# GLA scores with a 128 column stationary, decay logits with 128 rows, in a hybrid encoder step

## The chip, the cores and the metric

The kernel runs on one core of a Trainium2 chip. The metric is the device time of one execution in microseconds. Three runs of the kernel before took 977.99, 978.71 and 979.06 us, a median of 978.71. A further execution was profiled: it took 978.32 us.

The engines are named as the profile names them: PE is TensorE's matmul, PEld its load of the stationary operand, DVE VectorE, ACT ScalarE, POOL GpSimd, SP the engine that issues the DMAs.

## The reference

One layer over 2048 prompt frames (one stream) and 64 frames of a running stream, all in float32, model width 1024. RMSNorm, one input projection of 2832 columns, and then three groups whose outputs are gated, joined and sent through one output projection: banded attention (512 wide), gated linear attention or GLA (256) and a depthwise convolution of width 31 (256). The change is in GLA, which the reference writes in chunks of 64 frames:

```python
log_a = jax.nn.log_sigmoid((glr @ gla_w_up + gla_b).astype(jnp.float32)) / GLA_TAU
...
def step(S, inp):
    qc, kc, vc, gc = inp
    b = jnp.cumsum(gc, axis=1)
    b_last = b[:, -1:]
    q_t = qc * jnp.exp(b)
    k_t = kc * jnp.exp(-b)
    A = jnp.where(causal, jnp.einsum('bthd,bshd->bhts', q_t, k_t), 0.0)
    o = jnp.einsum('bhts,bshv->bthv', A, vc) + jnp.einsum('bthd,bhdv->bthv', q_t, S)
    k_end = kc * jnp.exp(b_last - b)
    S = jnp.exp(b_last[:, 0])[..., None] * S + jnp.einsum('bshd,bshv->bhdv', k_end, vc)
    return S, o
```

There are 4 heads with 32 key and 64 value columns each. `glr` has 16 columns. The first line is the "logits of the decay", `A` the "scores".

## The kernel before

The program for each engine is written by hand in its order, with semaphores between them; nothing is planned by a scheduler. Products in float32 are split: an operand becomes a high and a low part in a reduced format (names in `hi`/`lo`, `h`/`l`), and three matmuls stand for one. The small products of GLA aren't split; each is one float32 matmul, which the profile shows as two records on PE and two on PEld.

There are two passes. Pass A (up to about 480 us) does attention for 17 tiles of 128 frames and writes its part of the output. Pass B does GLA and the convolution in eight blocks b = 0 to 7 of 256 frames. Block 0 also carries the 64 frames of the running stream as a third tile, so it is 320 wide. In pass B of block b, TensorE does in this order (`for b in range(NB + 1)`, L2132 to L2215):

- the projections for the convolution (`project_b`, L1805) and for the values (`project_v`, L1958), with transposes of the block before between them,
- `gg` j = 0, the low-rank transpose `lowrank_T` (L2065), `gg` j = 1, then `gate_logits` (L2074), then `cg` and `pointwise` (L2055), `gk`, `gq`,
- the output of the block before in four halves (`output_b`, L1973, twelve matmuls each), and between them `kend_T` (L2081), `scores` for tiles 0 and 1 (L2098 and L2101), `state_update` (L2111) and `gla_o` (L2124, L2127).

A tile holds two chunks. `scores(b, i)` makes both chunks' scores of tile i for all 4 heads, in one bank of 512 columns: the left 256 for the first chunk (64 query columns a head), the right 256 for the second, whose stationary operand holds the keys of both chunks. The keys stand in `kb[128, 2, 5, 64]`, five groups of 64 columns for each tile: group 0 has the first chunk's keys for the first chunk's queries, groups 1 and 2 both chunks' keys for the second's, groups 3 and 4 those for the state. For the first chunk only 64 keys matter, so its stationary has 64 columns and its output 64 rows. VectorE's `mask_scores` then copies under a mask: rows 0 to 63 of the left half (L1624), all of the right half (L1627), and `gla_o` needs that (`a_masked`). The moving operand `qbd` has each head's queries in its own 32 rows and zeros elsewhere, so one matmul serves four heads.

`gate_logits` multiplies `wup` (16 rows of weights, one of bias) with `glrT`, the 17 rows of the transposed low-rank part with its row of ones. ScalarE puts these there (`take_lowrank`, L1122). `glrT` is the upper part of `bb`, where VectorE later writes the block's sums of the decay, all 128 rows (L1580). `wup` is a view of the packed parameters, which are in memory with 128 rows, zero below the 17th.

GpSimd clears some tiles once, ahead of block 0 (L881 to L885), and counts them on `zeros_b`; PE (L2061), ACT (L1230), DVE (L1740) and GpSimd itself (L916) wait for this count.

VectorE's order in a block is set by the convolution: 62 taps (L1478, L1482), cut into portions, with the steps of GLA, the adds of the output (`add`, L1653) and the split of the next block's input (L524) between them.

Of the kernel before, what the change touches and what calls it, by code (L numbers as in the profile page):

```python
# [25 lines left out]
ACT = mybir.ActivationFunctionType  # L26
# [7 lines left out]
P = 128  # L34
# [3 lines left out]
DEC = 64  # L38
CHUNK = 64
# [4 lines left out]
GH, GK, GV, LR = 4, 32, 64, 16  # L44
# [39 lines left out]
PARAMS, N_PARAMS = {}, 0  # L84
for _name, _width, _rows in (("reset", WIDE // 4, P), ("mask", P, P), ("wpw", CJ * CD, P), ("convw", CJ * CW, P),
                             ("convp", 3 * CJ, P), ("uh", CJ * HIST, P), ("glagain", 1, P), ("bpw", CJ, P),
                             ("wup", P, LR + 1), ("sts", GH * GV, P)):
    PARAMS[_name] = (N_PARAMS, _width, _rows)
    N_PARAMS += _width

# [25 lines left out]
def width(b):  # L116

    return WIDE if b == 0 else 256


def groups(b):

    if b < 0 or b >= NB:
        return []
    return [(0, 0, 256, (0, 1)), (1, 256, DEC, (2,))] if b == 0 else [(b + 1, 0, 256, (0, 1))]
# [7 lines left out]
def tiles(b):  # L133

    return [i for _, _, _, own in groups(b) for i in own]
# [59 lines left out]
def build(nc, ins, consts, x_T, outs):  # L195
# [7 lines left out]
    def sb(name, shape, dt=F32, ctx=es):  # L203
        return ctx.enter_context(nc.sbuf_tensor(name, shape, dt))

    def sem(name):
        return es.enter_context(nc.semaphore(name))

    with es:
# [68 lines left out]
        bb = sb("bb", [P, WIDE])  # L278
# [11 lines left out]
        zm = sb("zm", [P, WIDE])  # L290
        ez = sb("ez", [P, WIDE])
        qt = sb("qt", [P, WIDE])
        glrT = bb[0:LR + 1, :]
        e1, e2, e3 = qt, zm, ez
        eL = sb("eL", [P, 5])
        dec = sb("dec", [P, 3])
        kb = sb("kb", [P, 2, 5, 64])
        kbs = sb("kbs", [P, 2, 64])
        qbd = sb("qbd", [P, GH, WIDE])
# [21 lines left out]
        wup, glagain, bpw, sts = part("wup"), part("glagain"), part("bpw"), part("sts")  # L321
# [5 lines left out]
        T = [es.enter_context(nc.psum_tensor(f"T{i}", [P, 512], F32)) for i in range(3)]  # L327
# [40 lines left out]
        consts_a, consts_b, zeros_a, zeros_b = sem("consts_a"), sem("consts_b"), sem("zeros_a"), sem("zeros_b")  # L368
# [21 lines left out]
        gv_taken, lr_psum, lr_T = sem("v_taken"), sem("lowrank_psum"), sem("lowrank_T")  # L390
# [301 lines left out]
        def on_y(g):  # L692

            gi, _, w, own = g
            buf = on[:, own[0]:own[-1] + 1, :].rearrange("p i n -> p (i n)")
            return buf[:, 0:CJ * w].rearrange("p (j n) -> p j n", n=w)
# [143 lines left out]
        def _(pool):  # L840
# [42 lines left out]
            nc.gpsimd.memset(qbd[:, :, :], 0.0).then_inc(zeros_b, 1)  # L883
            nc.gpsimd.memset(glr1[:, :, LR:LR + 1], 1.0).then_inc(zeros_b, 1)
            nc.gpsimd.memset(eps_3[:, :], EPS).then_inc(zeros_b, 1)  # L885

            def o_rinv(g):
                gi, _, w, own = g
                a, e = own[0] * GH, own[-1] * GH + GH
                rows = slice(0, min(w, P))  # L890
                pool.wait_ge(go_ss, gi + 1)
                need(pool, go_n, gi)
                nc.gpsimd.tensor_tensor(oms[rows, a:e], oss[rows, a:e], eps_h[rows, a:e], ALU.add).then_inc(go_ms, 1)  # L893
                pool.wait_ge(go_ms, gi + 1)
                nc.gpsimd.tensor_tensor(orr[rows, a:e], oms[rows, a:e], mhalf[rows, a:e], ALU.pow).then_inc(go_r, 1)
# [17 lines left out]
                pool.wait_ge(gate_mul, at + 1)  # L913
                nc.gpsimd.tensor_tensor(dst, dst, graw[n % 2][:, 0:w], ALU.add).then_inc(gate_done, 1)

            pool.wait_ge(zeros_b, 5)  # L916
            for b in range(NB + 1):
                for g in groups(b - 1) if b < NB else []:
                    o_rinv(g)
# [11 lines left out]
        def _(act):  # L931
# [155 lines left out]
            def o_square(g):  # L1087
                gi, _, w, own = g
                rows = slice(0, min(w, P))
                bank = T[0] if own == (2,) else S[1]  # L1090
                act.wait_ge(go_psum, go_count(g))
                need(act, cnT_psum, groups_before(max(gi - 1, 0)))
                nc.scalar.activation(on[rows, own[0]:own[-1] + 1, :], bank[rows, 0:256 * len(own)].rearrange(
                    "p (i n) -> p i n", n=256), ACT.Square).then_inc(go_sq, 1)
# [24 lines left out]

            def take_lowrank(b):  # L1120
                act.wait_ge(lr_psum, b + 1)
                nc.scalar.activation(glrT[:, 0:width(b)], T[0][0:LR + 1, 0:width(b)], ACT.Copy).then_inc(lr_T, 1)  # L1122

            def log_decay(b):
                w = width(b)
# [58 lines left out]
            for b in range(NB + 1):  # L1184
                cur, done = b < NB, groups(b - 1) if b < NB else []
                for g in done:
                    o_square(g)
                if cur and b > 0:
                    glu_tanh(b, 0)
                    glu_tanh(b, 1)  # L1190
                if b == 1:
                    act.wait_ge(A.out_psum, 2 * TILES)
                    split_hi(B, OUT_HI, OUT_HI + 2)
                for g in done:
                    y_hi(g, on_y(g), ybg, 4.0, yg_ready, yg_hi)
                for i in tiles(b):
                    take_v(b, i)
                    if (b, i) == (0, 0):
                        split_hi(B, 5 * STAGES, 6 * STAGES)
                if b == 0:  # L1200
                    act.wait_ge(A.y_lo, 2 * TILES)
                    split_hi(B, 3 * KT, 4 * KT)
                if cur:
                    take_gate(b, 0)
                    take_lowrank(b)
                for g in done:
                    if g[3] != (2,):
                        conv_silu(g)
                if cur:
                    take_gate(b, 1)  # L1210
                    log_decay(b)
                for g in done:
                    if g[3] == (2,):
                        conv_silu(g)
                if cur:
                    if b == 1:
                        split_hi(B, OUT_HI + 2, OUT_HI + 4)
                    take_gate(b, 2)
                    decays(b)
                    if b == 1:  # L1220
                        split_hi(B, OUT_HI + 4, OUT_HI + 6)
                    take_gate(b, 3)
                    if b == 1:
                        split_hi(B, OUT_HI + 6, OUT_HI + 8)
                for g in done:
                    y_hi(g, cl[:, :, g[1]:g[1] + g[2]], ybc, 0.25, yc_ready, yc_hi)
                if cur:
                    take_kend(b)
                    if b == 0:
                        act.wait_ge(zeros_b, 5)  # L1230
                    q_blocks(b)
                if b == NB - 1:
                    g = groups(b)[0]
                    conv_silu(g)
                    o_square(g)
                    y_hi(g, cl[:, :, 0:256], ybc, 0.25, yc_ready, yc_hi)
                    y_hi(g, on_y(g), ybg, 4.0, yg_ready, yg_hi)
                if b + 1 < NB:
                    split_pair_hi(b + 1, 0)
                    split_pair_hi(b + 1, 1)  # L1240
# [3 lines left out]
        def _(dve):  # L1244
# [416 lines left out]
            for b in range(NB + 1):  # L1661
                p = b - 1
# [74 lines left out]
                if cur:  # L1737
                    taps(7)
                if b == 0:
                    dve.wait_ge(zeros_b, 5)  # L1740
                if prev:
                    add(p, 0, 1)
                if cur:
# [45 lines left out]
        def _(pe):  # L1789
# [268 lines left out]

            def lowrank_T(b):
                if b == 0:  # L2060
                    pe.wait_ge(zeros_b, 5)  # L2061
                pe.wait_ge(gv_taken, 2 * (tile_no(b, 0) + len(tiles(b))))
                for i in tiles(b):
                    rows = DEC if i == 2 else P
                    last = nc.tensor.transpose(T[0][0:LR + 1, i * P:i * P + rows], glr1[0:rows, i, :],  # L2065
                                               ident[0:rows, 0:rows])
                last.then_inc(lr_psum, 1)
# [19 lines left out]
            def scores(b, i):  # L2087
                bank = S[0] if i == 1 else T[2]
                by_head = lambda ap: ap.rearrange("p (h n) -> p h n", n=CHUNK)
                pe.wait_ge(qbd_ready, b + 1)  # L2090
                if i == 0:
                    need(pe, yc_ready, groups_before(b))
                elif i == 1:
                    need(pe, cn_ready, groups_before(b))
                else:
                    pe.wait_ge(a_masked, 1)
                first = kbs[:, 0, :] if i == 2 else kb[:, i, 0, :]
                last = nc.tensor.matmul(by_head(bank[0:64, 0:256]), first, qbd[:, :, i * P:i * P + CHUNK], start=True,  # L2098
                                        stop=True)
                if i < 2:  # L2100
                    last = nc.tensor.matmul(by_head(bank[:, 256:512]), kb[:, i, 1:3, :].rearrange("p c n -> p (c n)"),  # L2101
                                            qbd[:, :, i * P + CHUNK:(i + 1) * P], start=True, stop=True)
                last.then_inc(a_psum, 1)
# [28 lines left out]
            for b in range(NB + 1):  # L2132
                p = b - 1
# [147 lines left out]
```

## Time and profile before

| | us |
|---|---|
| median of 3 runs | 978.71 |
| the profiled execution | 978.32 |
| its span | 976.5 |
| PE busy (share of the span) | 920.2 (94%) |
| PEld busy | 813.5 (83%) |
| DVE busy | 790.8 (81%) |
| ACT busy | 475.2 (49%) |
| POOL busy | 203.9 (21%) |

The span runs from the first to the last instruction of the profiled execution; the 1.8 us between it and the time lie around it. Shares of busy time are means over two quite different passes, so the place of the change has to be read in its own window. The chain that ended last is the page's way to say what set the end: from the last instruction back, at each step to whatever released it. `128*64` in a row is a stationary of 128 rows and 64 columns, `128x256` the moving operand. Starts on PE overlap: a matmul is issued before the one ahead of it has ended, so what a matmul costs is the distance from its start to the next start, which the chain's pieces give, and not its duration.

### The profile page before, as it was taken

The page shows a single profiled execution, that of the slowest core. Times are in us where ns is not written, and L with a number is a line of the kernel's source. Part 1 is how long each engine was busy: PE and PEld are TensorE (multiplying, and loading weights), DVE is VectorE, ACT ScalarE, POOL GpSimd, SP SyncE. Part 2 cuts the span into 40 slices and gives each one's busy share as a digit, 9 for nine tenths or more (in the row PEclk, how much of TensorE's full clock was granted, in tenths as well). Part 3 has the DMA queues.
Part 4 walks back from the last instruction along what each step waited for, and adds up shares of the span by engine and source line. Part 5 has one row for each costly group of instructions (what it writes and reads, how often), then busy time and mean ns, then how long its engine had stood idle before and what let it go on. Part 6 is the DMA issues. An engine that isn't in the chain of part 4 may idle for free.

```text
span 976.5 us, 15956 instructions
## 1 busy us (share of the span) xinstructions
PE 920.2 (94%) x5713; PEld 813.5 (83%) x5713; DVE 790.8 (81%) x1905; ACT 475.2 (49%) x1166; POOL 203.9 (21%) x250
## 2 busy tenths in 40 slices
PE   5889999999999999998988789999999999999987
PEld 4767888888888888887975777998989898998965
DVE  6778888888888888888897768778878888888984
ACT  7666666666666666776642152041423224142311
POOL 1332222222222222210030230120301112120310
PEclk9899999999999999998997899999999999999999
DMA  9532332222222332163502203212040211203021
GB/s 297 201 125 88 109 108 107 97 103 105 107 95 95 105 108 87 62 198 90 153 23 77 66 24 97 76 44 87 2 130 1 76 54 61 70 13 119 1 76 57
DMA packets 57839, 87.79 MB, mean 90 GB/s; under 512 B 10048, under 2 KB 34496, under 8 KB 57760
## 3 DMA queue, kind: packets, MB, share of 16 engines
q1 hardware_dynamic: 57760, 86.77, 27.4%
q8 instruction: 46, 0.75, 0.3%
q14 instruction: 33, 0.27, 0.1%
HBM read 60.21 MB, written 26.60 MB: 89 GB/s over the span
## 4 chain that ended last, share of the span: by engine, by line
PE 74%; DVE 14%; ACT 4%; issue 3%; DMA 3%; SPq 1%; POOL 1%; POOLq 0%; DVEq 0%; ACTq 0%
PE J L656 19%; PE J L1805 17%; PE J L1973 9%; PE J L671 9%; DVE acc L1482 6%; PE J L1958 3%; PE S L1860 3%; PE S L2127 1%; PE T L1895 1%; PE T L2055 1%; ACT sc L1004 1%; PE S L1918 1%; DMA x_normed_scratch<-xraw 1%; ACT whi L462 1%; PE J L1995 1%
## 5 line engine op out<-in xcount | busy, mean ns | idle before, releaser
L1482 DVE SCALAR_TENSOR_TENSOR acc<-ub,cwh,acc 128x256 f32<-128x256 f32 (+1 forms) x480 | 225.1, 533 | 0.2
L656 PE MATMUL J<-whi,xhi 128*128 128x512 f32 (+1 forms) x408 | 151.3, 371 | 10.0 <-DVE wlo L472 10.0
L1805 PE MATMUL J<-xbh,whi 128*128 128x256 f32 (+1 forms) x512 | 150.9, 295 | 4.5 <-issue 4.5
L656 PE MATMUL J<-wlo,xhi 128*128 128x512 f32 (+1 forms) x408 | 147.6, 362 | 0.0
L656 PE MATMUL J<-whi,xlo 128*128 128x512 f32 (+1 forms) x408 | 147.3, 361 | 0.0
L1805 PE MATMUL J<-xbl,whi 128*128 128x256 f32 (+1 forms) x512 | 146.9, 287 | 0.0
L1805 PE MATMUL J<-xbh,wlo 128*128 128x256 f32 (+1 forms) x512 | 146.8, 287 | 0.0
L1805 PEld LDWEIGHTS J<-xbh,whi 128*128 128x128 f32 x512 | 97.8, 191 | 7.6 <-issue 7.1
L1805 PEld LDWEIGHTS J<-xbl,whi 128*128 128x128 f32 x512 | 98.0, 191 | 0.2
L1805 PEld LDWEIGHTS J<-xbh,wlo 128*128 128x128 f32 x512 | 97.7, 191 | 0.0
L656 PEld LDWEIGHTS J<-whi,xhi 128*128 128x128 f32 x408 | 78.2, 192 | 20.8 <-DVE xlo L614 10.0
L656 PEld LDWEIGHTS J<-whi,xlo 128*128 128x128 f32 x408 | 78.0, 191 | 12.8
L656 PEld LDWEIGHTS J<-wlo,xhi 128*128 128x128 f32 x408 | 78.2, 192 | 10.6
L1004 ACT ACTIVATE sc<-sc,nmx 128x192 f32<-128x192 f32 x136 | 60.3, 446 | 10.4 <-DVE nmx L1302 10.3
L1296 DVE CUSTOM_DVE_ANT_0 sc<-S,bias,sinks 128x192 f32<-128x192 f32 (+2 forms) x136 | 50.2, 406 | 10.2 <-PE S L1860 10.2
L671 PE MATMUL J<-whi,yhi 128*128 128x512 f32 x136 | 56.4, 415 | 0.0
L671 PE MATMUL J<-wlo,yhi 128*128 128x512 f32 x136 | 53.7, 395 | 0.0
L671 PE MATMUL J<-whi,ylo 128*128 128x512 f32 x136 | 53.6, 394 | 0.0
L604 POOL TENSOR_TENSOR xraw<-xraw,rb 128x1024 f32<-128x1024 f32 x17 | 40.8, 2400 | 51.4 <-ACT rb L598 51.4
L893 POOL TENSOR_TENSOR oms<-oss,eps_h 128x8 f32<-128x8 f32 (+1 forms) x9 | 4.9, 549 | 179.9 <-DVE oss L1495 179.0
L1958 PE MATMUL J<-whi,xbh 128*128 128x272 f32 x136 | 40.6, 298 | 0.4 <-DVE ub L1260 0.4
L1805 PE MATMUL J<-xbh,w2hi 128*128 128x256 f32 (+1 forms) x128 | 37.6, 294 | 3.1 <-ACT cgate L1118 3.1
(270 smaller groups left out, 2264.7 us busy)
## 6 DMA issues: line engine op xcount, KB each, us to landing
out<-res SPq DMA_DIRECT2D x60, 256.0 KB, 2.0
x_normed_scratch<-xraw SPq DMA_DIRECT2D x17, 512.0 KB, 2.9
xraw<-xT SPq DMA_DIRECT2D x16, 512.0 KB, 3.5
xtok<-in_x_prompt SPq DMA_DIRECT2D x16, 512.0 KB, 3.6
res<-in_x_prompt SPq DMA_DIRECT2D x16, 512.0 KB, 4.5
xbraw<-x_normed_scratch SPq DMA_DIRECT2D x16, 512.0 KB, 5.2
res<-out SPq DMA_DIRECT2D x14, 512.0 KB, 4.2
wraw<-in_w_in SPq DMA_DIRECT2D x52, 128.0 KB, 2.5
```

The lines of the kernel that those rows point to most:

```text
L462: nc.scalar.activation(weights(col, width)[0], stage(stage_of(ps, n))[:, 0:width], ACT.Copy, scale=scale).then_inc(ps.whi, 1)
L604: nc.gpsimd.tensor_tensor(xraw[t.par][:, :, :], xraw[t.par][:, :, :], rb[:, :].unsqueeze(1).to_broadcast([P, KT, P]), ALU.mult).then_inc(x ...
L656: last = nc.tensor.matmul(bank[:, 0:width], x[x_slot(ps, t)][:, k, :], w, start=(k == 0 and n == 0), stop=(k == KT - 1 and n == 2))
L671: last = nc.tensor.matmul(bank[:, :], y[:, k, :], w, start=(k == 0 and n == 0), stop=(k == 3 and n == 2))
L1004: last = nc.scalar.activation(unit(u), unit(u), ACT.Exp, bias=nmx[:, u:u + 1], accum_out=esum[:, u:u + 1])
L1296: nc.vector.tensor_tensor_reduce(out=unit(u)[:, cols], in0=S[n % 2][:, c * BAND:(c + 1) * BAND][:, cols], in1=bias[:, n, cols], scale=1.0, ...
L1482: nc.vector.scalar_tensor_tensor(acc[:, j, 0:frames], src, w, acc[:, j, 0:frames], ALU.mult, ALU.add).then_inc(conv_step, 1)
L1805: last = nc.tensor.matmul(bank[:, 0:w], wt, x[:, k, 0:w], start=(k == 0 and m == 0), stop=(k == KT - 1 and m == 2))
L1860: last = nc.tensor.matmul(S[n % 2][:, c * BAND:(c + 1) * BAND], qT[:, n, c, :, :].rearrange("p e q -> p (e q)"), band(t, n // 2, o, c), st ...
L1895: last = nc.tensor.transpose(T[2 * g][:, c * 256 + n % 2 * P:c * 256 + n % 2 * P + P], sc[:, n, c * 256:c * 256 + P], ident[:, :])
L1958: last = nc.tensor.matmul(bank[:, 0:B.widths[1]], x[:, k, at:at + P], wt, start=(k == 0 and m == 0), stop=(k == KT - 1 and m == 2))
L1973: last = nc.tensor.matmul(bank[:, :], y[:, k % 2, at:at + P], wt, start=(k == 0 and m == 0), stop=(k == 3 and m == 2))
```

## The change

The first chunk's scores of tiles 0 and 1 get a stationary of 128 columns, groups 0 and 1 of `kb`, and write 128 rows instead of 64. Rows 64 to 127 of the left half then hold products that nobody reads. The third tile of block 0 keeps 64 columns.

The logits take all 128 rows of `wup` and of `bb`. Rows 17 to 127 of `wup` are zero. Those of `bb` must hold finite numbers: GpSimd clears `bb` once, and from block 1 on it holds the sums of the block before. The count on `zeros_b` goes from 5 to 6, and ScalarE waits for it in block 0 before it writes `bb`. No other instruction is added, none changes its place, and no transfer changes.

```diff
@@ -84,7 +84,7 @@
-                             ("wup", P, LR + 1), ("sts", GH * GV, P)):
+                             ("wup", P, P), ("sts", GH * GV, P)):
@@ -290,7 +290,7 @@
-        glrT = bb[0:LR + 1, :]
+        glrT = bb[:, :]
@@ -883,6 +883,7 @@
             nc.gpsimd.memset(eps_3[:, :], EPS).then_inc(zeros_b, 1)
+            nc.gpsimd.memset(bb[:, :], 0.0).then_inc(zeros_b, 1)
@@ -913,7 +914,7 @@
-            pool.wait_ge(zeros_b, 5)
+            pool.wait_ge(zeros_b, 6)
@@ -1119,7 +1120,9 @@
                 act.wait_ge(lr_psum, b + 1)
-                nc.scalar.activation(glrT[:, 0:width(b)], T[0][0:LR + 1, 0:width(b)], ACT.Copy).then_inc(lr_T, 1)
+                if b == 0:
+                    act.wait_ge(zeros_b, 6)
+                nc.scalar.activation(glrT[0:LR + 1, 0:width(b)], T[0][0:LR + 1, 0:width(b)], ACT.Copy).then_inc(lr_T, 1)
@@ -1227,7 +1230,7 @@
-                        act.wait_ge(zeros_b, 5)
+                        act.wait_ge(zeros_b, 6)
@@ -1737,7 +1740,7 @@
-                    dve.wait_ge(zeros_b, 5)
+                    dve.wait_ge(zeros_b, 6)
@@ -2058,7 +2061,7 @@
-                    pe.wait_ge(zeros_b, 5)
+                    pe.wait_ge(zeros_b, 6)
@@ -2094,8 +2097,9 @@
-                first = kbs[:, 0, :] if i == 2 else kb[:, i, 0, :]
-                last = nc.tensor.matmul(by_head(bank[0:64, 0:256]), first, qbd[:, :, i * P:i * P + CHUNK], start=True,
+                rows = slice(0, DEC if i == 2 else P)
+                first = kbs[:, 0, :] if i == 2 else kb[:, i, 0:2, :].rearrange("p c n -> p (c n)")
+                last = nc.tensor.matmul(by_head(bank[rows, 0:256]), first, qbd[:, :, i * P:i * P + CHUNK], start=True,
                                         stop=True)
```

## Rows read from the trace of the kernel before

**Rows 1.** The page, part 4: shares of the chain that ended last, by engine.

```profile
PE 74%; DVE 14%; ACT 4%; issue 3%; DMA 3%; SPq 1%; POOL 1%; POOLq 0%; DVEq 0%; ACTq 0%
```

**Rows 2.** Sums by window: length, busy us of PE, PEld, DVE, ACT, POOL, clock.

```profile
540.00:592.42 52.42, 41.63 (x293) 39.68 (x291) 38.71 (x85) 17.86 (x43) 17.21 (x16) 0.87 0.13 45
592.42:648.06 55.64, 55.64 (x371) 50.21 (x372) 43.71 (x104) 15.75 (x36) 7.74 (x10) 1.00 0.22 67
703.68:759.30 55.62, 55.62 (x396) 51.22 (x396) 46.05 (x109) 16.93 (x39) 9.47 (x12) 1.00 0.19 58
870.54:905.00 34.46, 34.46 (x231) 30.77 (x231) 28.09 (x67) 6.48 (x13) 3.87 (x4) 1.00 0.31 93
905.00:951.00 46.00, 42.00 (x279) 37.47 (x277) 41.49 (x97) 13.36 (x34) 11.85 (x12) 0.96 0.12 41
```

**Rows 3.** The chain in order of time (start us, us, what), outside the gapless stretch.

```profile
568.64 1.75 DVE acc L1482 x2
...
910.68 7.92 DVE acc L1482 x20
...
935.93 4.58 PE J L1973 x12
...
940.72 2.77 PE J L1973 x12
943.49 0.58 PE T L2098 x2
```

**Rows 4.** The chain in block b = 3.

```profile
715.16 0.57 PE T L2098 x2
715.73 0.63 PE T L2101 x2
716.36 0.58 PE S L2098 x2
...
720.33 0.86 PE T L2111 x4
...
748.34 2.84 PE J L1805 x24
751.18 0.62 PE T L2074 x2
751.81 3.04 PE J L1805 x24
```

**Rows 5.** Groups by shape, weight loads: shapes, count | busy us, mean ns | idle before.

```profile
L2101 PEld LDWEIGHTS T<-qbd,kb 128*128 128x128 f32 x16 | 2.4, 188 | 3.1 <-issue 3.1
...
L2074 PEld LDWEIGHTS T<-bb,params 17*128 17x128 f32 x16 | 2.3, 182 | 3.0 <-ACT bb L1122 2.0
...
L2098 PEld LDWEIGHTS T<-qbd,kb 128*64 128x64 f32 x16 | 1.5, 135 | 3.5 <-issue 2.5 <-ACT qbd L1155 1.0
```

**Rows 6.** Time line (start us, us, instruction, idle before): GpSimd's memset, transpose L2065.

```profile
480.27 0.31 POOL L881 MEMSET stp<- 128x256 f32 x1 [23.97 <-DVE ylo L1265]
...
493.34 0.86 POOL L912 TENSOR_TENSOR ggate<-ggate,graw 128x320 f32<-128x320 f32 x1 [10.68 <-ACT ggate L1118]
...
487.55 0.54 PE L2065 MATMUL T<-ident,glr 128*17 128x128 f32 x3
```

**Rows 7.** Time line, b = 0: the taps ahead of the masks, TensorE behind them.

```profile
519.88 2.05 DVE L1482 SCALAR_TENSOR_TENSOR acc<-ub,cwh,acc 128x350 f32<-128x350 f32 x4
...
522.76 0.67 PE L2124 MATMUL S<-stp,qt 128*128 128x256 f32 x2 [0.32 <-DVE asb L1627]
```

**Rows 8.** Time line, b = 7: the last mask, the transpose L2028.

```profile
947.53 0.43 DVE L1627 COPY_PREDICATED asb<-params,S 128x256 f32<-128x256 uint8 x1
...
948.50 0.60 PE L2028 MATMUL S<-ident,acc 128*128 128x128 f32 x4
```

**Rows 9.** Time line, b = 3: the state update and the matmul that reads it.

```profile
722.97 1.15 DVE L1639 SCALAR_TENSOR_TENSOR stp<-stp,dec,T 32x64 f32<-32x64 f32 x4
...
725.12 0.59 PE L2124 MATMUL S<-stp,qt 128*128 128x256 f32 x2
```

## The prediction, made before the kernel ran

> **What bounds the kernel now.** I read the page's chain first, then the sums by window, then the chain in order of time, then single instructions. On the page 74% of the chain that ended last runs on TensorE [rows 1]. Both edits act in the second half only (the mixer pass with its GLA part, eight blocks b = 0 to 7), so the question is in which blocks TensorE is the bound. The sums by window answer it. From 592.42 to 905.00 us TensorE is busy in every microsecond of every window, at a granted clock of 1.00. A block repeats in 55.62 us there, with 46.05 us of work for VectorE [rows 2]; the first, a middle and the last of six such windows stand there. Before it (b = 0, and b = 1 up to its output) and behind it (b = 7) TensorE has gaps [rows 2], and the chain runs through VectorE's convolution taps L1482, which cover the logits of b = 1 (the piece at 568.64 us) as those of b = 7 (the piece at 910.68) [rows 3].
>
> In one gapless block (b = 3) every piece of the chain is TensorE's. Five of them belong to this change: the scores L2098, L2101, L2098, L2101 with 0.57 + 0.63 + 0.58 + 0.63 = 2.41 us (the fourth repeats the second), and the logits of the decay, L2074, with 0.62 [rows 4]. What these take from start to start comes off the 55.62 us, if nothing else arrives late.
>
> **What a narrow or a short stationary costs.** The nearest full operation is L2111 (128 rows, 128 columns, 256 moving, float32): two matmuls in 0.86 us, 0.43 each [rows 4]. L2101 has exactly this shape and takes 0.63, though it waits for no semaphore; it only follows a matmul of 128*64. L2098 has half the columns to load, 135 ns against 188, and takes 0.57. The load queue shows where this goes. A load normally lies under the matmul before it. Before the loads of tile 0 of these two lines the queue stood idle for 3.5 + 3.1 = 6.6 us, and only 1.0 of it was a wait for another engine [rows 5]. So each change between a 64 column and a 128 column stationary uncovers a load and adds a pause.
>
> **Edit 1, scores with 128 columns** (tiles 0 and 1 of each block; the third tile of b = 0 keeps its 64). It takes 2.41 us out and puts four full matmuls in, 4 x 0.43 = 1.72. Saved: 0.69 us a block. Nothing in the trace shows a full load ahead of a full L2101, so I bound it: above, by L2111's 0.43 for all four; below, by 4 x 0.63 = 2.52, L2101 as it is now, a loss of 0.11 (rival C goes further). I take 0.43, since L2111 is the nearest in shape and type and L2101's only difference is what stands before it. The upper 64 rows that are now written are read by nobody, VectorE masks the same 64 rows as before, no instruction is added.
>
> **Edit 2, logits with 128 rows.** L2074 loads 17 rows and 128 columns. Its piece is 0.62 against 0.43: 0.19. The 24 matmuls behind it take 3.04 against 2.84 for the 24 ahead of it: 0.20 [rows 4]. The chain follows no other engine here, so this isn't a wait for ScalarE. Saved: 0.39 us a block; the bound from below is 0.00 (the load alone grows from 182 ns to 188 [rows 5]).
>
> Here two rules of the Trainium skill stand against each other. "TensorE: Matmul & The Clock Gate", section LDWEIGHTS, has a load paid by its columns and not by its rows: by that alone edit 2 gives nothing, and edit 1 makes each narrow load some 53 ns longer. The loads themselves agree with it (182 ns for 17 rows, 188 for 128, 135 for 64 columns), and it is what rivals A and C rest on. "TensorEngine Tiling (Array Packing)", section Key Properties, has TensorE drained whenever the tiling mode changes; by that both edits pay. The gaps around L2101 and L2074 agree with it, and it has no price.
>
> **What is added.** One memset of `bb`, 128x320, on GpSimd. That of `stp`, 128x256, took 0.31, so about 0.4 us. GpSimd was free 10.68 us before 493.34, at 482.66, so it ends near 483.1. The first that waits for the higher count is TensorE's transpose L2065, at 487.55 [rows 6]: 4.4 us of cover. ScalarE's new wait, ahead of the logits' input of b = 0, comes later still. I take both at 0; with the cover gone it is 0.4 us once.
>
> **In which blocks it counts.**
> - b = 2 to 6, both edits, no gap: 5 x (0.69 + 0.39) = 5.40 us.
> - b = 1: the scores lie in the gapless stretch, 0.69. Its logits lie beside taps that set the pace, 0 [rows 3].
> - b = 0: VectorE masks the scores after the taps that end at 521.93, and TensorE waits 0.32 us for the mask [rows 7]. 0 for both.
> - b = 7: the logits lie beside taps, 0. The scores are on the chain (943.49) [rows 3]. But the transpose L2028, at 948.50, also waits for the masks of both tiles, which VectorE ends at 947.53 + 0.43 = 947.96, at the pace of its taps and not of the scores [rows 8]. So it can come no earlier than about 948.05 and gains 0.45 of the 0.69. What follows moves with it.
>
> Sum: 5.40 + 0.69 + 0.45 = 6.54 us. The profiled execution took 978.32 us with a span of 976.5, which would become 971.8 and 970.0. The median of the runs shown, 978.71, is 0.39 above that execution; with it I get **972.2 us**.
>
> **What is late next.** The closest is VectorE's state update of tile 0, L1639. It ends at 722.97 + 1.15 = 724.12, and L2124, which reads it, starts at 725.12 [rows 9]. Of this 1.00 us the scores take 0.69, and 0.31 is left if VectorE doesn't move at all. It will move, since adds of the output ahead of it wait for TensorE. No new wait, but it is tight, and the next gain there would find it.
>
> **Rivals.**
> - A: rows don't matter. If 17 rows of stationary can be followed by 128 without a pause, and L2074's gaps have another cause, edit 2 gives nothing: 972.2 + 5 x 0.39 = 974.1 us. For it: its neighbours have the same 128 columns. Against it: 3.04 against 2.84 behind it, with no wait recorded. 12%.
> - B: VectorE takes over. If L1639 comes later than I think (its work falls together with GpSimd's in another way), six blocks give back about half of 0.69: 2.1 us, 974.3. For it: the slack of 0.31. Against it: VectorE has 9.6 us without work in a block. 5%.
> - C: slower. The pause comes not from the change of shape but from this strided `qbd` behind unrelated matmuls, and stays; then all that changes is the load. 188 - 135 = 53 ns, uncovered, four loads a block (two lines, two records), seven blocks on the chain: 1.5 us. Edit 2 then pays nothing either: 980.2 us. It decides as soon as the load isn't laid under the matmul ahead. For it: L2101's own loads are uncovered now. Against it: L2111, full and float32 too, runs at 0.43. 4%.
> - D: the clock. In b = 7 the first twelve L1973 take 4.58 us and the next twelve 2.77 [rows 3], after a gap, and this window has a granted clock of 0.96 [rows 2]. With other arrival times one such fall can be added, or this one can be missed: 1.8 us either way, 974.0 or 970.4. 6% for the worse.
>
> **Numbers.** My forecast has 73%, A 12, B 5, C 4, D 6. Faster by over 0.2% (2 us, about what a measurement of this kernel tells from none) means below 976.7, where all but C lie: faster 0.93, same 0.05, slower 0.02. The range reaches up past A, B and D (974.0 to 974.3) and leaves C out. Down it takes D's other sign with b = 7 at its full 0.69, 970.4 - 0.2. So 970.2 to 974.5.
>
> **What would show it.** L2098 and L2101 stand as 128*128, and the chain's pieces of scores sum to 1.7 us a block. L2074 is a 128*128 piece of 0.43 with 2.84 for the 24 behind it. A gapless block lasts 54.54 us, and the stretch before 592.4 keeps its length. L2028 of b = 7 waits for masks. I am wrong if L2101 stays at 0.63 (C), if L2074 keeps its gaps (A), or if TensorE waits for `stp` between 592 and 900 us (B).

## The result, and the profile after

The changed kernel takes 971.44 us (median of 4 runs, 970.4 to 973.35) against 978.88 (977.99 to 979.1) for the kernel before: a ratio of 0.9923, interval 0.9907 to 0.9939. The forecast was 972.2 us in a range of 970.2 to 974.5. A second sample of the changed kernel (e7) and the first together have a median of 972.55 over 12 runs.

The profiled execution took 970.40 us with a span of 968.6, 7.9 less than the span before. First the sums by window, cut at steps of one block from the start of the output of b = 1, in the columns of [rows 2] (after the clock come the busy share of the DMA engines and their GB/s):

```profile
540.00:591.00 51.00, 41.65 (x300) 40.09 (x298) 37.48 (x85) 17.86 (x44) 18.11 (x16) 0.90 0.13 45
591.00:645.53 54.53, 54.53 (x371) 50.75 (x372) 43.61 (x103) 15.67 (x36) 7.59 (x10) 1.00 0.22 68
700.07:754.60 54.53, 54.53 (x397) 51.78 (x396) 46.02 (x108) 16.85 (x39) 9.43 (x12) 1.00 0.19 59
863.65:898.11 34.46, 34.46 (x238) 32.00 (x236) 28.45 (x69) 6.48 (x13) 3.99 (x4) 1.00 0.30 92
898.11:944.00 45.89, 41.36 (x277) 38.07 (x276) 41.76 (x100) 13.36 (x34) 12.30 (x12) 0.96 0.12 41
```

The block without gaps lasts 54.53 us instead of 55.62. TensorE is still busy in all of it; its weight loads are busy for longer (51.78 against 51.22 us a block) in a shorter block, so the time did not come from less loading. The chain of b = 3 (start us, us, what) says where it came from:

```profile
711.56 0.43 PE T L2102 x2
711.99 0.43 PE T L2105 x2
712.42 0.43 PE S L2102 x2
712.85 0.43 PE S L2105 x2
...
744.05 2.84 PE J L1808 x24
746.89 0.43 PE T L2077 x2
747.32 2.83 PE J L1808 x24
```

These are the lines of [rows 4], three or four further down in the code. All four pieces of scores take 0.43 us, the figure of L2111, where they took 0.57 and 0.63. The logits take 0.43 for 0.62, and the 24 matmuls behind them 2.83 for 3.04. The groups of weight loads by shape show the gaps closed (busy us, mean ns | idle before):

```profile
L2105 PEld LDWEIGHTS T<-qbd,kb 128*128 128x128 f32 x16 | 3.0, 190 | 0.4
L2102 PEld LDWEIGHTS T<-qbd,kb 128*128 128x128 f32 x16 | 3.0, 188 | 0.7
L2077 PEld LDWEIGHTS T<-bb,params 128*128 128x128 f32 x16 | 2.5, 190 | 2.4 <-ACT bb L1125 2.4
```

L2102 now needs 188 ns to load instead of 135, and the queue stood idle 0.7 us before its sixteen loads instead of 3.5 [rows 5]. Before L2077 it was idle for 3.0 us, 2.0 of it a wait for ScalarE; what is left now is such a wait alone (2.4). The longer load costs nothing, since it lies under the matmul ahead again. Then b = 7, in the chain:

```profile
903.13 7.92 DVE acc L1485 x20
...
928.38 4.58 PE J L1976 x12
...
939.75 0.33 DVE asb L1627
940.08 0.34 DVE asb L1630
940.42 0.14 issue
940.55 0.63 PE S L2031 x4
```

The transpose L2031 waits for the last mask, as forecast. From the start of the output (928.38, before 935.93) to it (940.55, before 948.50 [rows 8]) 12.17 us pass instead of 12.57: a gain of 0.40.

The new memset of `bb` took 0.37 us and is over at 482.37. TensorE's transpose L2068, the first that waits for the higher count, starts at 486.96, and GpSimd's own next instruction at 493.10:

```profile
482.00 0.37 POOL L886 MEMSET bb<- 128x320 f32 x1
```

### The profile page after: what moved, and what is told of

Same layout as the page of the kernel before. It is cut to its first block, busy times and chain, and to the rows that moved or that the text cites. A ratio compares the mean times of both kernels' runs of the same rounds, so it can differ in the third digit from the quotient of the medians.

```text
span 968.6 us, 15958 instructions
## 1 busy us (share of the span) xinstructions
PE 911.9 (94%) x5713; PEld 818.6 (85%) x5713; DVE 789.7 (82%) x1905; ACT 474.2 (49%) x1166; POOL 204.9 (21%) x251
## 4 chain that ended last, share of the span: by engine, by line
PE 74%; DVE 13%; ACT 5%; DMA 3%; issue 3%; SPq 1%; POOL 1%; POOLq 0%; DVEq 0%; ACTq 0%
PE J L656 19%; PE J L1808 18%; PE J L671 9%; PE J L1976 8%; DVE acc L1485 6%; PE J L1961 3%; PE S L1863 3%; PE S L2131 1%; PE T L1898 1%; DMA wraw<-in_w_in 1%; PE T L2058 1%; ACT sc L1005 1%; ACT whi L462 1%; DMA x_normed_scratch<-xraw 1%; PE S L1921 1%
```

## The experiments

All medians are device us; one execution of each is profiled, and the length of a block is read in it from the start of one `kend` transpose (`kend_T`) to the next. The kernel before had a median of 978.90 to 979.14 us beside each group.

**One edit alone.** e1 has the full width scores and the short logits of before; e2 the reverse.

```diff
e1 (against before)
+                rows = slice(0, DEC if i == 2 else P)
+                first = kbs[:, 0, :] if i == 2 else kb[:, i, 0:2, :].rearrange("p c n -> p (c n)")
+                last = nc.tensor.matmul(by_head(bank[rows, 0:256]), first, qbd[:, :, i * P:i * P + CHUNK], start=True,
...
e2 (against before)
+                              ("wup", P, P), ("sts", GH * GV, P)):
...
+        glrT = bb[:, :]
...
+            nc.gpsimd.memset(bb[:, :], 0.0).then_inc(zeros_b, 1)
```

> Edit 1 alone. My theory (each change of shape between 64 and 128 columns costs about 0.1 us and uncovers a load): 0.69 us a block in b = 1 to 6, 0.4 in b = 7, so 4.5 us, a time of 974.3; a gapless block lasts 54.93 us. The 1.4 us that the changed kernel gained before 591 us in its profile stay away if they come from the logits of b = 1 (start of the output of b = 1 near 592.4 us, as before), and come if they are chance. Rival C (narrow operands cost by themselves, wider ones 53 ns more each): 980 us. Rival A says nothing here.

> Edit 2 alone. My theory: 0.39 us in each of b = 2 to 6, 1.95 us, a time of 976.9, a gapless block of 55.23 us. If in b = 1 the shorter logits let VectorE go on before GpSimd gets in (two taps of 0.95 us become 0.47 us), another 1.0 us: 975.9, with the output of b = 1 starting near 591.0 us. Rival A (rows don't matter): 978.9, gapless block 55.62.

e1: 975.51 us (6 runs), ratio 0.9965, interval 0.9951 to 0.9979; a block lasts 54.93 us, 0.69 less. e2: 978.74 us (12 runs), ratio 1.0003, interval 0.9991 to 1.0015; a block lasts 55.23 us, 0.39 less. So in the block the two gains are exactly the two terms of the forecast, and they add to the 1.09 of the changed kernel. In the whole time e1 stays 1.2 us behind the 974.3 expected, and the logits alone bring nothing that can be told (978.74 for an expected 976.9), though their profile has the 5 x 0.39 = 1.95 us. The chain of e2 shows one place where time goes back:

```profile
748.99 0.43 PE T L2077 x2
749.42 2.83 PE J L1808 x24
...
932.55 5.41 PE J L1976 x12
```

The logits have their full gain. But the first twelve L1976 behind the gap of b = 7 take 5.41 us, where the profiles of before and of the changed kernel have 4.58: the granted clock is at its lower level for longer there. This isn't a mark of e2: the second profile of the changed kernel (e7, below) has 5.46. So the medians need a count over all runs. Over 24 runs of e2 and e6 (e6 has 96 rows, and the same block as e2), the time at half clock, worked out from each run's mean clock and span, is 49.1 us on average. It is 44.6 in 64 runs of before, 45.6 in 12 of the changed kernel, 47.7 in the 6 of e1, with errors of the mean of 1.0, 0.5, 1.4 and 0.9. Within one kernel a run takes about 0.3 us longer for each us more at half clock. By this estimate the clock accounts for some 1.3 of the 1.95, and for some 0.9 of the 1.2 us that e1's 3.4 lacks of 6 x 0.69 + 0.45 = 4.6. The rest is inside the intervals. Why the clock is low for longer in e2 and e6 than in before stays open, and whether the changed kernel differs from them in this isn't clear.

Both expectations also asked where the changed kernel's first profile got 1.42 us before the output of b = 1. That output starts at 592.72 us in e1 and at 589.43 in e2 (592.42 before, 591.00 in the changed kernel), which by their words speaks for the logits; it is taken up below with the other runs.

**Is it the number of changes of shape?** e3 keeps both narrow scores but issues them next to each other (wide, narrow, narrow, wide), so that a block has two changes between a narrow and a full stationary there instead of four.

```diff
+                for part in {0: (wide, narrow), 1: (narrow, wide), 2: (narrow,)}[i]:
+                    last = part()
```

> The kernel before, with no operand widened, only the order of the two score matmuls of tile 0 turned round: wide, narrow | narrow, wide instead of narrow, wide | narrow, wide. There are two changes of shape left of four. My theory (the change costs, not the narrow operand): the start-to-start distances that fall away are 0.10 at the first, 0.05 and 0.05 inside the narrow ones or 0.09 and 0.10 between, 0.35 us a block in all, seven blocks: 2.4 us, 976.4; a gapless block of 55.27 us. Rival C (the narrow or strided operand costs by itself): no change, 978.9, 55.62.

978.07 us (12 runs), ratio 0.9989, interval 0.9977 to 1.0001: 2.4 us were expected, and the whole time shows some 1 that can't be told from none. The block is 55.28 us, 0.34 shorter, half of 0.69, as expected. Its chain in b = 3 shows which of the four scores are still dear, those behind a stationary of the other width:

```profile
714.69 0.43 PE T L2103 x2
715.12 0.58 PE T L2099 x2
715.70 0.43 PE S L2099 x2
716.13 0.63 PE S L2103 x2
```

One load of each kind is covered again (idle before sixteen loads, as above):

```profile
L2103 PEld LDWEIGHTS T<-qbd,kb 128*128 128x128 f32 x16 | 3.0, 188 | 0.7
...
L2103 PEld LDWEIGHTS S<-qbd,kb 128*128 128x128 f32 x16 | 2.4, 188 | 3.1 <-issue 3.1
L2099 PEld LDWEIGHTS S<-qbd,kb 128*64 128x64 f32 x16 | 2.2, 137 | 1.3
L2099 PEld LDWEIGHTS T<-qbd,kb 128*64 128x64 f32 x16 | 1.5, 134 | 2.7 <-issue 2.7
```

The two that follow one of their own shape (128*128 in T behind full matmuls, 128*64 in S behind the other 128*64) have little idle time before them. So the price belongs to the change of shape, in either direction, and not to the narrow operation: 0.34 us for two changes, 0.17 each, and 0.39 for the two around the logits.

**Which sizes are a change of shape?** e4 gives the scores 96 columns (short logits); e5 and e6 give the logits 64 and 96 rows (narrow scores).

```diff
e4 (against before)
+                rows = slice(0, DEC if i == 2 else 96)
+                first = kbs[:, 0, :] if i == 2 else kb[:, i, 0:2, :].rearrange("p c n -> p (c n)")[:, 0:96]
...
e5 (against e2; e6 with 96)
-        glrT = bb[:, :]
+        glrT = bb[0:64, :]
```

> The kernel before, with a stationary of 96 columns for the first chunk's scores instead of 64 or 128. If what counts is whether the operand fits into a part of the array (64 columns do, 96 don't), 96 is as good as 128: 0.69 us a block, 974.3 us, starts 0.43 us apart, with loads of some 160 ns. If what counts is that both stationaries have the same number of columns, 96 costs as 64 does: 978.9.

> Edit 2 alone, but with 64 rows of the stationary instead of 128 (17 before). My theory: an operand of 64 rows still takes only a part of the array, so it costs as 17 rows do: the piece 0.62 us, the 24 matmuls behind it 3.04, a gapless block of 55.62 us, and a time as before (978.9). If the cost comes from few rows as such and falls with each row, about half of 0.39 is gained: 55.4.

> The same with 96 rows, which no half of the array holds. My theory: it costs as 128 rows do, the piece is 0.43 us and a gapless block 55.23 us. The other theory (falls with each row): near 55.3, between 64 and 128 rows. On the time: the logits alone gave 978.74 (0.16 less than before) although their profile shows 1.96 us less in the gapless blocks. If that missing 1.8 us was chance of the half-clock stretches and start-up, this run, the same kernel but for the rows, shows 976.9; if something takes it back each time, 978.7 again.

e4: 977.06 us (10 runs), ratio 0.9969, interval 0.9952 to 0.9986; block 54.92 us, the whole gain of e1, though the time is 2.8 us above the 974.3 expected (its profiled execution took 970.47). e5: 978.37 (12 runs), ratio 1.0, interval 0.9987 to 1.0014; block 55.62 us, no gain at all. e6: 979.40 (12 runs), ratio 1.0002, interval 0.9985 to 1.002; block 55.24 us, the gain of e2. The expectation of e6 had set 976.9 against 978.7: that speaks against chance in e2's twelve runs. The chains of e5 and then of e6 in the logits of b = 3:

```profile
754.35 0.63 PE T L2077 x2
754.98 3.03 PE J L1808 x24
```

```profile
747.57 0.43 PE T L2077 x2
748.00 2.84 PE J L1808 x24
```

64 rows are as dear as 17, 96 as cheap as 128, and likewise for 64 and 96 columns. The load's own length has no part in it: 184 ns for 64 rows, 190 for 96. Sizes between 64 and 96 weren't tried.

**Sample again, and the mask of b = 7.** e7 is the changed kernel with no edit. e8 puts VectorE's second output addition of b = 7 behind the four masks, since L2031 waits for the last of them.

```diff
+                if prev and b < NB - 1:
                     add(p, 0, 1)
...
+                if prev and b >= NB - 1:
+                    add(p, 0, 1)
```

> The changed kernel once more, for a second profile and more times. My theory: gapless block 54.53 us, from the transpose of keys of b = 1 to the end 6.5 us less than before, 972.2 us, and the start of the output of b = 1 within 1 us of 592.4 on the average. If the 1.4 us that its first profile gained before 591 us belong to the edits, they are there again, and the time is 971.0.

> The changed kernel with one add of the output (tile 0, second half) put behind the masks of the scores in b = 7. If in b = 7 the transpose of the convolution waits for the masks, as forecast, it comes 0.3 us earlier relative to the scores: from the start of the scores to the start of the transpose 4.5 us instead of 4.79, and the end follows. If it waits for something else, nothing moves. The time alone can't tell (0.03%).

e7: 973.11 us (8 runs), ratio 0.9944, interval 0.9926 to 0.9963; block 54.53 us again. Two other parts of what was expected weren't met. The output of b = 1 starts at 589.95 us, 2.5 ahead of 592.4. And from the `kend` transpose of b = 1 to the end it takes 377.2 us, 4.0 less than the 381.2 before and not 6.5. What is missing lies in b = 7, in TensorE's work at the lower clock:

```profile
928.84 5.46 PE J L1976 x12
...
955.09 1.12 PE T L2014 x4
956.21 9.33 PE J L1998 x36
```

The first profile of the same kernel has 4.58, 0.66 and 8.46 us there. This is rival D, 2.2 us for the worse, with no edit between the two executions.

e8: 972.73 (4 runs), ratio 0.9942, interval 0.9921 to 0.9964. From the `kend` transpose of b = 7 to the end e8 takes 35.53 us and the changed kernel 35.82. The chain of e8 runs through TensorE alone here, without the masks:

```profile
938.92 2.76 PE J L1978 x12
941.68 0.44 PE S L2033 x4
942.12 0.86 PE T L2117 x4
```

So the 0.3 us that the scores of b = 7 saved and the masks kept back are to be had. A run can't tell them from nothing; the profile can.

**A version that beats both.** The comparison of before and after had shown taps of VectorE at two lengths, 468 ns and 947 ns, the long ones next to GpSimd's work on the gates (next section). e9 moves the gates of b = 0 and b = 7 to VectorE, one instruction for GpSimd's two. e10 has e8's swap as well.

```diff
+            def gate_dve(b, n):
+                if b not in (0, NB - 1):
+                    return
...
+                nc.vector.scalar_tensor_tensor(dst, dst, 1.0, graw[n % 2][:, 0:w], ALU.add, ALU.mult).then_inc(gate_done, 1)
```

> The changed kernel with the gates of b=0 and b=7 moved from GpSimd to VectorE, one (in + 1) * gate instruction each; GpSimd keeps those of b=1 to b=6, so that its work no longer lies beside the taps of the first and the last block. Theory of sharing: a VectorE tap takes 950 to 960 ns (1195 to 1245 at 350 wide) while GpSimd's gate instructions run and 468 (570) otherwise; eight taps of b=0 and eight of b=7 are slow in the changed kernel and stand on VectorE's way to the output. Without GpSimd beside them b=0 gains 8 x 0.6 less 4 x 0.5 = 2.9 us, b=7 gains 8 x 0.49 less 4 x 0.42 = 2.2 us, 5 us in all, about 967.5 us against 972.6 of the changed kernel, and the slow taps of both blocks are gone. Rival: the taps are slow there for another reason (their operands, the DMAs that run then); VectorE just gets eight instructions more, about 3.7 us, and the kernel is slower than the changed one.

> The kernel of e9 with the last block's masks ahead of one output addition on VectorE as in e8 as well. Both gains stand at different places (the taps of b=7, and the step from its scores to the transpose of the masked scores), so they should add: 0.3 us under e9, about 967.2 us by the theory of sharing. Rival: with the taps of b=7 quicker, the masks are no longer what the transpose waits for, and the swap brings nothing over e9.

e9: 963.62 us (962.51 to 964.47, 5 runs), ratio 0.9847, interval 0.983 to 0.9864: 15.5 us under the kernel before and 8.9 under the pooled 972.55 of the changed kernel, where 5 were expected. e10: 965.86 (961.29 to 966.44, 5 runs), ratio 0.9854, interval 0.9831 to 0.9876, which isn't told from e9; from the `kend` transpose of b = 7 to the end it takes 35.50 us against 35.82 in e9, so the swap brings its 0.3 here too. Two pieces of the chain of b = 7, in the changed kernel and then in e9:

```profile
911.65 3.51 DVE acc L1485 x4
...
920.15 6.76 DVE acc L1485 x13
```

```profile
908.17 1.59 DVE acc L1487 x4
...
910.47 0.42 DVE ggate L1586
...
914.24 0.40 DVE ggate L1586
...
915.43 4.82 DVE acc L1487 x13
...
920.97 0.34 DVE cgate L1586
...
922.05 3.01 PE J L1991 x12
```

The taps give 1.92 + 1.94 = 3.86 us, the 8 x 0.49 expected, and three gates cost 1.16 of it. What the expectation lacked is the last row: the first twelve matmuls of the output in b = 7 take 3.01 us instead of 4.58, since the granted clock isn't low there in e9, nor in e10. That makes 4.3 of the 4.4 us by which b = 7 shrank between these two profiles (60.8 us from `kend` to `kend` became 56.3). b = 0 and the start of b = 1 gave 3.5 for the 2.9 expected; this part varies by as much from one execution to the next.

## Why the prediction was right, step by step

**The sum by blocks.** With the `kend` transposes as marks, the first profiled pair divides as follows:
- from `kend` of b = 1 to that of b = 6, which holds the scores of b = 1 to 5 and the logits of b = 2 to 6 (five times both edits): forecast 5.40, measured 283.63 - 278.19 = 5.44 us.
- from there to `kend` of b = 7, the scores of b = 6: forecast 0.69, measured 61.45 - 60.76 = 0.69.
- b = 7, scores held back by the masks: forecast 0.45, measured 36.19 - 35.82 = 0.37 to the end of the kernel, 0.40 to L2031. The mechanism is the one named; e8 shows it by taking it away. The size was 0.05 to 0.08 too large, since L2031 starts 0.14 us behind the last mask and not 0.1.
- before the gapless stretch (b = 0 and the start of b = 1): forecast 0, measured 1.42 us in this pair.

The three terms add to 6.50 us, against a forecast of 6.54, and the medians of all runs (978.9 and 972.6) differ by 6.4. The last line is the one miss. Most of it is a pair of taps, seen on VectorE and GpSimd in the time line, of before and then of after:

```profile
566.12 3.11 POOL L912 TENSOR_TENSOR ggate<-ggate,graw 128x256 f32<-128x256 f32 x1 [3.79 <-ACT ggate L1118]
568.57 1.82 DVE L1482 SCALAR_TENSOR_TENSOR acc<-ub,cwh,acc 128x256 f32<-128x256 f32 x2
569.31 0.79 POOL L914 TENSOR_TENSOR ggate<-ggate,graw 128x256 f32<-128x256 f32 x1
```

```profile
565.39 4.24 POOL L913 TENSOR_TENSOR ggate<-ggate,graw 128x256 f32<-128x256 f32 x1 [3.47 <-ACT ggate L1119]
568.17 0.86 DVE L1485 SCALAR_TENSOR_TENSOR acc<-ub,cwh,acc 128x256 f32<-128x256 f32 x2
569.71 0.74 POOL L915 TENSOR_TENSOR ggate<-ggate,graw 128x256 f32<-128x256 f32 x1
```

In the piece that [rows 3] show at 568.64, two taps took 1.82 us. GpSimd's first multiplication ends during the first of them (at 569.23), and its addition L914 lies beside the second. In the changed kernel the multiplication ends only at 569.63, behind both taps, and they took 0.86. This is 0.96 of the 1.42. Whether it is due to the edits the runs don't decide. All five executions with 96 or 128 rows of logits (the changed kernel, e2, e6, e7, e8) have the pair fast. Of the five with fewer, before and e1 have it slow, and e3, e4 and e5 fast. So the short logits alone don't make it slow. Nor is 1.42 us a measure of anything: in these ten executions the output of b = 1 starts anywhere from 587.5 (e4) to 594.0 us (e5).

**What was luck.** The sum is right in the gapless stretch in both profiles of the changed kernel. That the first pair also agrees outside it is in part luck: 1.42 us gained ahead of the stretch, and no fall of the clock added in b = 7. The second profile has 2.2 us of the latter. Its own eight runs have a median inside the range (973.11), but single runs reach from 970.19 to 977.35.

**The bounds.** I had taken L2111's 0.43 for all four scores, with a loss of 0.11 as the other end. The nearest full operation was the right row to go by: it is 0.43 to the last digit. The memset at 0, with 0.4 us to pay if its cover were gone, stood as well (0.37, covered).

**The rules weighed.** The trace, e5 and e6 settle between the two. The load lasts as its columns say and hardly as its rows (182 ns with 17 rows, 184 with 64, 190 with 96 or 128, against 135 with 64 columns), as the Trainium skill has it in "TensorE: Matmul & The Clock Gate", section LDWEIGHTS; but its length isn't what is paid. "TensorEngine Tiling (Array Packing)" of the Trainium skill, section Tiling Modes, lists modes of 64 and 32 rows and of 64 and 32 columns and none of 96, and has TensorE drained when the mode changes. The runs agree on every size tried: 17 and 64 rows and 64 columns pay, 96 rows and 96 columns don't.

**The rivals.** A (rows don't matter) asked for L2077 to keep its gaps; they closed, and e2 without the other edit shows 0.39 a block. Its 974.1 us is too near to the medians measured to be refuted by them; the block refutes it. B asked for a wait for `stp` in the gapless stretch; TensorE has none, and the blocks there are equal to 0.01 us. C asked for the pause to stay, as a trait of the strided `qbd`; with the same `qbd` it is gone in the changed kernel and in e4, and half gone in e3. D (the clock, 1.8 us) is real in size: it is absent in the changed kernel's first profile (the same 4.58 us for the first twelve L1976 of b = 7), and takes 2.2 us in its second. Of the ten executions profiled with the gates on GpSimd, e2, e3, e6 and e7 have 5.4 to 5.5 us there, the others 4.3 to 4.6. The mean clock of the 64 runs of before spreads as well, from 0.972 to 0.983, so a ratio of medians over many runs is hurt less by it than a pair of profiles.

## What to carry to other kernels

A small operand on TensorE is not free of charge because it loads faster. In a stretch that TensorE bounds, where one of 17 or 64 rows or of 64 columns stands between full ones, widen it to 96 or 128 (with zeros or unread rows), or put the small ones next to each other; each change of shape cost 0.17 to 0.2 us here. Price such an edit by the length of the gapless block, not by the median: the medians' intervals were 2 to 3.5 us wide, and an edit with a certain 1.95 us was not seen in it. Profile the same kernel twice before a difference outside that block is put down to an edit. Before going on with TensorE, look at how long the same instruction of VectorE takes at different places: here a factor of two, with GpSimd beside it, was worth more than the whole change.

## What was not expected of the hardware

**Two lengths of one instruction.** A tap (two inputs and one output in SBUF) takes 466 to 489 ns, or 946 to 971 where GpSimd's instructions on the gates come between; at 350 wide 580 on average in e9, and 1181 to 1248 beside GpSimd in the changed kernel. GpSimd's multiplication suffers as well, by its records, which are rough: while taps follow without a gap it doesn't end, and they stay fast (the 4.24 us above; 4.48 in b = 7, for a shortest of 0.73). Once it has ended, the taps beside GpSimd's next instructions are slow. Without GpSimd beside them (e9) all of the slow taps of b = 0 and b = 7 are gone. The Trainium skill, "SBUF — State Buffer", section "SBUF: two separate sides", has VectorE and GpSimd share a pair of ports that one instruction holds alone while the other waits, for a VectorE instruction with two inputs in SBUF too. In b = 7 of the changed kernel the four slow taps start every 0.88 us (3.51 for four), and so do GpSimd's instructions beside them (912.33, 913.08 and 914.08 us). That agrees with such a use by turns; no run tries it apart from the operands.

**A narrow operand that costs nothing.** The transposes of `glr` have a stationary of 17 columns between full ones, and stand in the chain of the changed kernel at 0.22 us for two, the same as two transposes with 128 columns:

```profile
708.59 0.22 PE T L2084 x2
...
743.39 0.22 PE T L2068 x2
```

The Trainium skill, "TensorEngine Tiling (Array Packing)", section Restrictions, says that column tiling turns off the transpose mode for float32; a transpose would then run untiled, whatever its columns. No run here widened these transposes, so that this is the reason is argued and not shown.

**The clock differs between executions of one kernel.** The time at the lower clock behind the gap of b = 7, from the granted clock by window, is 3.4 us in the profiles of before, e1, e4, e5, e8 and the first of the changed kernel, 6.8 in e2, e3, e6 and in the second of the changed kernel (e7), and none in e9 and e10. The first twelve matmuls there take 4.58 us (changed kernel), 5.46 (e7) and 3.01 (e9). So a profile can show 0.9 us for the worse or 1.6 for the better at a place that an edit doesn't touch, and between e7 and the first profile there is no edit at all. Whether e9's shorter taps are what keeps the clock up there, or chance, two profiles (e9 and e10) don't prove.
